# A prompt's expert slots in two halves of 64, beside the sample's mixers

## The reference, cut to what matters

```python
def trunk_layer(x, mod, p, ...):
    h = rmsnorm(x, p['norm1_w']) * (1.0 + sc1) + sh1
    u = h @ p['w_in']
    ...                                        # four mixers side by side
    x = x + g1 * (y @ p['w_out'])
    h2 = rmsnorm(x, p['norm2_w']) * (1.0 + sc2) + sh2
    return x + g2 * peer(h2, ...)

def peer(x, w_q, sub_keys, u_tab, v_tab):      # per token: 8 heads x 16 experts = 128 slots
    q = x @ w_q                                # 8 heads, two halves of 128
    s = q . sub_keys                           # 128 scores per head and half
    s_top, i_top = top_k(s, 16)
    best, pos = top_k(s_top[0] + s_top[1], 16) # over the 16 x 16 sums
    idx, gate = expert numbers of the 128 slots, softmax(best)
    act = gelu(sum_d u_tab[idx] * x)           # one row of 1024 per slot
    return sum_slots (gate * act) * v_tab[idx]
```

## Time and profile before

| | |
|---|---|
| three executions, median (lowest to highest) | 2624.39 us (2620.61 to 2626.53) |
| the profiled execution, its own time | 2637.35 us |
| its span, first to last instruction | 2635.6 us |
| mean granted TensorE clock | 0.831 |
| PE, DVE, ACT, POOL busy | 1741.6, 1563.3, 372.9, 1452.5 us |
| moved by DMA | 959.35 MB, 364 GB/s on average |
| of it by GpSimd's gathers | 805.40 MB |

### The profile page before, as it was taken

How to read it: one execution, slowest core, us unless ns; L and a number is a source line. 1 busy time by engine, 2 the same in 40 slices (tenths; PEclk the granted TensorE clock), 3 DMA queues, 4 the chain that set the end, 5 groups by cost and what they waited for, 6 DMA issues and landing times.

```text
span 2635.6 us, 27950 instructions
## 1 busy us (share of the span) xinstructions
PE 1741.6 (66%) x10250; PEld 1070.4 (41%) x10250; DVE 1563.3 (59%) x4010; ACT 372.9 (14%) x917; POOL 1452.5 (55%) x1540
## 2 busy tenths in 40 slices
PE   6979598778984011079888699868991000088888
PEld 5858477746634011044244188746641000011111
DVE  2314899851689999931108279981499999900000
ACT  3322132121111000010111132211110000000000
POOL 0000455443566676757765645443567777777775
PEclk8989799878996555589999999978995555599999
DMA  9488599766999999999999989866999999999999
GB/s 395 160 326 319 219 421 345 259 227 235 405 410 420 420 420 420 420 361 412 403 415 420 388 330 375 286 226 231 376 411 381 420 420 420 420 420 419 412 420 371
DMA packets 249495, 959.35 MB, mean 364 GB/s; under 512 B 32400, under 2 KB 33680, under 8 KB 231568
## 3 DMA queue, kind: packets, MB, share of 16 engines
q0 software_dynamic: 221184, 805.40, 77.1%
q1 hardware_dynamic: 19584, 142.62, 13.6%
q10 hardware_dynamic: 8592, 9.56, 1.0%
HBM read 955.11 MB, written 2.36 MB: 363 GB/s over the span
## 4 chain that ended last, share of the span: by engine, by line
POOL 26%; PE 24%; DVE 23%; DMA 13%; issue 10%; ACT 2%; ACTq 0%; SPq 0%; POOLq 0%; DVEq 0%
POOL sb_ring L561 26%; PE pb L584 18%; DVE sb_ring L2001 10%; DMA sb_ring<-in_peer_v,sb_idxT 6%; DMA sb_ring<-in_peer_u,sb_idxu 5%; PE pv L584 5%; DMA sb_wring<-in_w_in_blocks 1%; PE pb L587 1%; DVE sb_i16u L1881 1%; DVE sb_big L1572 1%; ACT sb_big L1127 1%; DMA sb_ring<-in_w_mod_blocks 1%; DVE sb_xe L1877 1%; ACT sb_hT L1127 1%; DVE sb_big L1694 1%
## 5 line engine op out<-in xcount | busy, mean ns | idle before, releaser
L561 POOL DMA_INDIRECT sb_ring<-in_peer_u,sb_idxu x768 | 724.7, 944 | 698.7 <-DVE sb_idxT L1969 293.7
L561 POOL DMA_INDIRECT sb_ring<-in_peer_v,sb_idxT x768 | 727.6, 947 | 469.8 <-issue 210.2
L2001 DVE CUSTOM_DVE_ANT_0 sb_ring<-sb_ring,pv 128x1024 f32<-128x1024 f32 x768 | 907.7, 1218 | 29.9 <-DMA sb_ring<-in_peer_u,sb_idxu 22.9
L584 PE MATMUL pv<-sb_ring,sb_wcol 128*32 128x512 f32 x3072 | 645.7, 616 | 75.5 <-DMA sb_ring<-in_peer_v,sb_idxT 67.3
L584 PE MATMUL pb<-sb_hT,sb_wring 128*128 128x256 f32 (+1 forms) x1920 | 372.3, 354 | 49.8 <-ACT sb_big L1127 26.4
L584 PEld LDWEIGHTS pb<-sb_hT,sb_wring 128*128 128x128 f32 x1920 | 319.5, 201 | 122.8 <-issue 73.5
L584 PEld LDWEIGHTS pv<-sb_ring,sb_wcol 128*32 128x32 f32 x3072 | 125.1, 110 | 542.4 <-DMA sb_ring<-in_peer_v,sb_idxT 367.5
L587 PE MATMUL pb<-sb_cst,sb_dots 128*128 128x128 f32 x6 | 2.4, 402 | 409.6 <-DVE sb_dots L2007 409.6
L584 PE MATMUL pb<-sb_big 128*128 128x128 f32 (+1 forms) x1696 | 202.7, 281 | 17.7 <-DVE sb_big L1690 14.2
L584 PEld LDWEIGHTS pb<-sb_big 128*128 128x128 f32 (+1 forms) x1696 | 192.4, 192 | 32.5 <-DVE sb_big L1690 18.0
L2038 DVE TENSOR_TENSOR sb_big<-pv,sb_big 128x512 f32<-128x512 f32 x4 | 2.7, 687 | 318.0 <-PE pv L584 318.0
(11 more groups left out here) (240 smaller groups left out, 1690.0 us busy)
## 6 DMA issues: line engine op xcount, KB each, us to landing
sb_ring<-in_w_mod_blocks SPq DMA_DIRECT2D x38, 1024.0 KB, 7.0
sb_wring<-in_w_in_blocks SPq DMA_DIRECT2D x34, 1024.0 KB, 7.8
sb_wring<-in_w_q_blocks SPq DMA_DIRECT2D x26, 1024.0 KB, 8.0
sb_wring<-in_w_out_blocks SPq DMA_DIRECT2D x14, 1024.0 KB, 7.7
sb_ring<-in_peer_u,sb_idxu POOLq DMA_INDIRECT x768, 10.2
sb_ring<-in_peer_v,sb_idxT POOLq DMA_INDIRECT x768, 8.1
sb_wring<-in_w_mod_blocks SPq DMA_DIRECT2D x10, 1024.0 KB, 7.2
sb_ring<-in_w_in_blocks SPq DMA_DIRECT2D x6, 1024.0 KB, 14.3
```

Source lines behind the costliest of these rows:

```text
L561: pool.indirect_dma_start(ring[:, j, :], None, a["tab_" + kind][l_of(q)], bass.IndirectOffsetOnAxis(ap=of, axis=0)).then_inc(rows_in[j], 16)
L584: return nc.tensor.matmul(out, lhsT, rhs, start=start, stop=stop)
L2001: dve.tensor_tensor_reduce(out=row, in0=row, in1=pv[:, :, :].rearrange("p a b -> p (a b)"), scale=1.0, scalar=0.0, op0=ALU.mult, op1=ALU.a ...
```

## The change

For q 0 and 3, the prompt's blocks, a part is half of the slots: 64 u gathers, then 64 v gathers of which each serves two tokens (64 slots of one on the lower partitions, 64 of the other on the upper), then the other half in the same way. A v item still is four gathers, now of eight tokens; the weight column of a gather has two columns of `wcol`, with zeros where the other token's slots are. The gelu, the weight transposes, the operand copy into `pv` and `item_end` come once for each half. The prompt's expert numbers of the first half are written as soon as the second quarter is there, and the weave of the sample's units is another. The sample's blocks keep their parts of 128.

```diff
+def parts_of(q):
+    return 2 if q in (0, 3) else 1
+def rows_of(q):
+    return SLOTS // parts_of(q)
+def steps_of(q):
+    return rows_of(q) // STEP
...
 SAMPLE_WEAVE = {
-    "norm1": ([1], 1), "proj": ([1, 1, 0, 1, 1, 0, 1, 0, 1, 0, 0, 1, 0, 1, 0, 1, 0, 1, 0], 1),
-    "intra0": ([1, 1, 0, 1, 1, 1, 1, 1, 1, 0], 0), "intra1": ([1, 1, 0, 1, 1, 1, 0, 1, 1, 0], 0),
-    "scan": ([1, 0, 0, 1, 0, 0, 1, 0], 0), "fnet": ([], 1), "attp": ([1, 1], 0), "att0": ([0, 2, 0], 0), "att1": ([0, 2, 0], 0), "out": ([0, 0, 0, 1, 0, 0, 1], 0),
-    "query": ([3] + [0, 1, 1, 1] * 2 + [1, 1, 1, 1] * 2, 1), "topk0": ([5], 0), "topk1": ([1], 0)}
+    "norm1": ([1], 1), "proj": ([1, 0, 1, 0, 1, 0, 1, 0, 1, 0, 1, 0, 1, 1, 0, 1, 0, 1, 0], 1),
+    "intra0": ([0, 1, 0, 1, 0, 1, 0, 0, 0, 0], 0), "intra1": ([0, 1, 0, 1, 0, 1, 0, 1, 0, 0], 0),
+    "scan": ([1, 1, 0, 1, 1, 0, 1, 1], 0), "fnet": ([], 1), "attp": ([1, 1], 0), "att0": ([0, 1, 1], 1),
+    "att1": ([1, 1, 1], 0), "out": ([0, 1, 1, 1, 1, 1, 1, 1], 0),
+    "query": ([1] + [1, 1, 2, 1, 0] + [1, 1, 1, 1] * 2 + [1, 1, 1], 1), "topk0": ([4], 0), "topk1": ([0], 0)}
...
-                if n < ahead or own[n][0] in ("gelu", "end", "modsum") and not isinstance(k, str):
+                if n < ahead or own[n][0] in ("gelu", "end", "modsum") and not isinstance(k, str) and k != ("query", 5):
...
-                    of = idxu[:, t, s:s + 1] if kind == "u" else idxT[:, t, token(s):token(s) + 1]
+                    at = rows_of(q) * part + s if kind == "u" or parts_of(q) == 2 else token(s)
+                    of = (idxu if kind == "u" else idxT)[:, t, at:at + 1]
...
-                                o = j * LANES + LANES - 1 - m
+                                o = j * LANES + LANES - 1 - m * parts_of(q)
...
+                if parts_of(q) == 2:                                   # ScalarE, item_gelu
+                    halves = wT[:, :].rearrange("p (n e) -> p n e", e=2)
+                    if part == 0:
+                        for e in range(2):
+                            s = slice(64 - 64 * e, P - 64 * e)
+                            fn(halves[s, :, e], zero[s].to_broadcast((64, 64)))
+                    act.wait_ge(*done("wT_full", (q, part)))
+                    for e in range(2):
+                        s = slice(64 * e, 64 * e + 64)
+                        last = fn(halves[s, :, e], pb[s, 2, 0:P].rearrange("p (n e) -> p n e", e=2)[:, :, e])
...
                 for k in range(4):                                     # DVE, st_query
-                    gap(u, "query", 4 * k + 4)
+                    gap(u, "query", 4 * k + 4 if k else 5)
...
+                    if k % 2 and nt == 1:
+                        dve.wait_ge(*stepped())
+                        q, t = seq_tiles(u)[0]
+                        dve.tensor_copy(idxu[:, t, slots_of(q, k // 2)], idxrow[:, k // 2, 0:64]).then_inc(*tick("idx_ready", (q, k // 2)))
+                        dve.tensor_copy(idxrow[:, k // 2, 64:128], idxrow[:, k // 2, 0:64]).then_inc(*(tick("idx_rows", u) if k == 3 else step()))
...
-                dve.tensor_copy(idxT[:, t, :], pb[:, 4, 0:P]).then_inc(*tick("idxT_copied", q))
+                if parts_of(q) == 1:                                   # DVE, st_topk
+                    last = dve.tensor_copy(idxT[:, t, :], pb[:, 4, 0:P])
+                else:
+                    for part in range(2):
+                        for e in range(2):
+                            s = slice(64 * e, 64 * e + 64)
+                            last = dve.tensor_copy(idxT[s, t, slots_of(q, part)].rearrange("p (m g) -> p g m", g=GROUPS),
+                                                   pb[s, 4, part * P:part * P + P].rearrange("p (g m e) -> p g m e", g=GROUPS, e=2)[:, :, :, e])
```

More of the change, by code:

```diff
@@ L276, in build @@
     for it in side + sched:
-        if it[0] in ("u", "v") and it[:2] not in phase_of:
-            v_before[it[:2]] = sum(k == "v" for k, _ in phase_of)
-            phase_of[it[:2]] = len(phase_of)
+        if it[0] in ("u", "v"):
+            key = (it[0], it[1], it[3])
+            if key not in phase_of:
+                v_before[key] = [(q, part) for kind, q, part in phase_of if kind == "v"]
+                phase_of[key] = sum(rows_of(q) for _, q, _ in phase_of)
     with ExitStack() as ctx:
@@ L453, in token, with rows_before, last_row, fills_before @@
             return s % GROUPS * LANES + s // GROUPS
-        def rows_before(phase):
-            return phase * SLOTS
+        def rows_before(kind, q, part):
+            return phase_of[kind, q, part]
+        def last_row(kind, q, part):
+            return phase_of[kind, q, part] + rows_of(q) - 1
+        def fills_before(q, part):
+            return sum(steps_of(x) for x, _ in v_before["v", q, part])
+        def slots_of(q, part):
+            return slice(rows_of(q) * part, rows_of(q) * part + rows_of(q))
         def landed(r):
@@ L1952, in quarter @@
                 two = hexp[:, :, 0:n].rearrange("p s (i h) -> p s i h", i=nt)
-                last = stt(idxrow[:, 0:nt, 32 * k:32 * k + 32], two[:, 0], float(NKEYS), two[:, 1], ALU.mult, ALU.add)
-                last.then_inc(*(tick("idx_rows", u) if k == 3 else step()))
+                new = idxrow[:, 0:nt, 32 * k:32 * k + 32] if nt == 2 else idxrow[:, k // 2:k // 2 + 1, 32 * (k % 2):32 * (k % 2) + 32]
+                last = stt(new, two[:, 0], float(NKEYS), two[:, 1], ALU.mult, ALU.add)
+                last.then_inc(*(tick("idx_rows", u) if nt == 2 and k == 3 else step()))
             def st_topk(u, i):
```

160 lines of the change are left out of this document (92 added, 68 removed).

## The result

The kernel after takes 2655.09 us (median of four runs, 2647.34 to 2659.07), the kernel before beside it 2625.46 (four runs, 2620.61 to 2627.42): the ratio is 1.0112, with a 95% interval of 1.0085 to 1.0139. That is 29.6 us more, where the prediction said 22. The profiled execution of after took 2655.02 us (span 2652.8), as its median; the one of before, 2637.35, lay 13 above the median of its other three.

The account below looks back on a forecast made before the run. Bound: the moment DVE has written the sample's expert numbers. Per mixer +10.3 us, twice 20.6, plus 3.8 index work, minus 2 early rows: +22 on 2637.35 gives 2659; shifted 13 lower to the median, 2646 us, range 2606 to 2670.

Parts of the forecast that it names:

- intra0: First intra stage: five of eight u items leave at 0.5 us each, about 1 more at level starts; -3.5 us.
- The gelu's wait: End of intra0: the first gelu now ends this stage, and intra1's decay matmuls stand behind its wait; +3.7 us.
- intra1, scan and fnet: intra1: seven u items leave, four v items enter, +4.2 us; scan and fnet: u items leave, seven v items enter, -12.
- The price of the u items: Scan and fnet: u items exposed there, with one on DVE ahead of attp, leave 12.8 us to gain.
- clock and waits: Scan: half of the 11.8 us that TensorE's products would save at the upper clock was taken as gain, 5.9 us.
- The clock's rival: Rival, chance 0.25: TensorE keeps full clock from intra1 to att0; scan and fnet give 25 instead of 12; 2611 us.
- att0 and att1: Attention stages: late v items, extraction of the first half's sum and DVE work before att1's scores cost +10.4 us per mixer.
- The sum with the operand copy: Between att0 and att1: sum extraction 3.8 us, some 1 overlapping; adding the half 1.1; operand copy 1.23; u item 4.7.
- out: Output projection: seven u items on DVE, each ahead of a residual step that frees a PSUM bank; +7.5 us.
- late rows: Rival, chance 0.10: second half's u rows arrive late, from att1 to query; 10 us more per mixer, 2666 us.
- query and search: Query: first scores come 5.6 us earlier, but five u items and the gelu precede DVE's first quarter; 0 us.
- Index work and early rows: Prompt units: extra copies and a transpose on DVE, +3.8 us for two units; first gathers up to 30 us earlier, -2.

Follow-up runs that it names:

- the second trace: The unchanged kernel before, profiled once more for a second trace; that execution took 2615.69 us.
- thin rows: Kernel before, with the last 16 of a prompt block's 128 u rows multiplied over 8 of 1024 columns; 2597.47 us, ratio 0.9905.
- the version meant to beat both: Kernel after with one PSUM sum for both halves, 12 of the second half's 16 u items before the first half's v rows; 2615.17 us, ratio 0.9972.
- the one with fewer in scan: The version meant to beat both, rewoven: three instead of six v items in scan, four early in query, second gelu later; 2621.41 us, ratio 0.9999.
- one sum alone: Kernel after, both halves' v rows summed in one PSUM tile, second half's u rows reading tokens from SBUF; 2644.59 us, ratio 1.0089.

## Why the prediction was right, and where it was not

The direction and the bound were right: the number that sets the time is the moment at which DVE has the sample's experts, and it moved by 16.3 and 12.8 us per mixer where +10.3 was forecast. By steps:

- **intra0**: -3.5 forecast, -3.9 in both units against the second trace (-6.6 / -5.2 against the first, from which the forecast was made). The gelu's wait that was booked here (+3.7) stands at the start of intra1: TensorE waits 2.76 us there for the weighted dots.
- **intra1, scan and fnet**, with that gelu: +4.2 + 3.7 - 12 = -4.1 forecast (12.8 - 6 + 5.9 is 12.7, and 12 was taken), -2.6 / -3.5 measured. The price of the u items was near (12.8; 10.4 / 7.4 in the stages with thin rows, 11 to 12.5 by the times). The two numbers behind it were both too small, and it is luck that their errors mostly cancel: the v items cost TensorE 11.9 / 11.7 us rather than 6, and clock and waits give back 9.3 rather than 5.9. The clock's rival was right about the clock (0.89 in scan) and wrong about the time, because the rise is paid for by the items that cause it.
- **att0 and att1**: +10.4 forecast. Measured +12.2 / +12.0 against the trace from which it was made, +15.7 / +13.1 against the second one: too low by 2 to 5. The path was seen rightly: from the end of att0's last product (565.52 in after) to DVE's reading of att1's scores (580.64) it is 15.1 / 15.2 us in after and 3.6 in both units of the first trace, so +11.5. The v items behind that product were priced 3.6: the version meant to beat both, which has two there, takes 6.3 / 6.1 for this stretch, the one with fewer in scan, which has none, 2.2, so they cost about 4. The sum with the operand copy, and the u item that stands ahead of the reading, was priced at 3.8 - 1 + 1.1 + 1.2 + (4.7 - 3.05) = 6.8 us; one sum alone takes 8.6 / 8.9 from this stretch (6.5 / 6.3 are left), because the u item runs beside the v items there. So of the sum's terms it is the extraction with the u item that was sized too small. Outside this stretch 0.7 / 0.4 us are left against the first trace and 4.2 / 0.1 against the second (whose unit 3 takes 2.2 us for the stretch). The attentions' own products take 20.8 us on TensorE in after, 19.7 / 20.0 in the first trace of before and 16.7 / 15.4 in the second, at other granted clocks. The prediction had no term for that, and no run shows how much of the 4.2 it is.
- **out**: +7.5 forecast, +9.0 / +7.7 measured, and only half the reason. It was priced as DVE's items ahead of the residual steps, with late rows as a rival of 10%. Both hold at once: either limit alone gives nearly the same length, and the 10 us more that late rows were to cost did not come.
- **query and search**: 0 forecast, -1.3 / +0.6 measured.
- **Index work and early rows**: +3.8 and -2 forecast. The early rows gave nothing (2648.47 without them); the index work is too small to be told from the starts of intra0 in unit 1, which lie between 386.8 and 393.1 us in the kernels with halves and between 388.1 and 395.0 in those without.

Against the second trace the mixers lost 29.1 us where 20.6 were forecast; 8.0 of the 8.5 between are att0 with att1. That the first profiled execution of before lay 13 us over the median hardly mattered, since the forecast was shifted to the median; but the first two traces alone would have shown a loss of 16.1 us in these stages, and the forecast would have seemed too high.

Unit 3 of the second trace of before has 4.4 us less in att0 and 7.2 more in att1 than its unit 1. That is the clock: 1.00 in the products of att0 and 0.66 in att1 (1766.2 to 1791.6 us), where unit 1 has 0.78 and 0.91; the attentions' own products take 6.2 and 9.2 us there, and 9.2 and 7.6 in unit 1. So single stages of attention can't be compared between two traces to better than some 4 to 7 us.

Left open: why the clock falls at other moments in the two units, and whether the version that beats both would gain more with its att0 items in the softmax wait alone, which was not tried without the change in query.

## What to carry to other kernels

Price a side item by the engine that is full in the stage it enters, not by what it costs there now: in a stage where two engines are nearly full, one item less gains little and one more costs all of it. Where work is moved into an idle engine, ask whether its data can arrive at that rate too; if compute and supply come to the same length, thinning out either one shows nothing, and only both together show where the time is. And what an early step gained here was worth nothing, ahead of a stretch in which TensorE and the transfers were nearly full already.
